# Seven products instead of eight for the other half of the second FFN product as well, with weight sums made in place

## The reference

```python
u = jnp.einsum('bsd,df->bsf', x, w_in)            # 2048 -> 2 * 5632
c = conv_b + up[:, 0:S] * conv_w[0] ...           # causal, width 3
g, val = jnp.split(c, 2, axis=-1)
return jnp.einsum('bsf,fd->bsd', jax.nn.gelu(g) * val, w_out)   # 5632 -> 2048
h = layer_norm(DEEPNORM_ALPHA * h + f, ...)
```

## Time and profile before

| what | value |
|---|---|
| median of three runs | 2568.05 us |
| the profiled execution's own time | 2568.06 us |
| its span | 2566.3 us |
| TensorE busy (matmul) | 2552.7 us, 99% of the span |
| VectorE busy | 1697.4 us, 66% |
| ScalarE busy | 1235.3 us, 48% |
| DMA | 496.05 MB, mean 193 GB/s |

### The profile page before, as it was taken

The page is one execution under the profiler, slowest core; times in us unless marked ns, Lnnn a source line. Parts: engine busy times, 40 slices in busy tenths (PEclk is TensorE's granted clock), DMA queues, the critical chain, the costliest instruction groups (busy, mean ns, idle before and its releaser), DMA issues.

```text
span 2566.3 us, 40343 instructions
## 1 busy us (share of the span) xinstructions
PE 2552.7 (99%) x14286; PEld 2227.7 (87%) x14286; DVE 1697.4 (66%) x1922; ACT 1235.3 (48%) x1383; POOL 15.9 (1%) x39
## 2 busy tenths in 40 slices
PE   9999999999999999999999999999999999999998
PEld 9999888888888888888888888888888888888887
DVE  6666667767666796565555555554766767678955
ACT  4444445555555554434444344433455555555532
POOL 0000000000000000000000000000000000000000
PEclk9999999999999999999999999999999999999999
DMA  7554574555555656655555555566555555556464
GB/s 280 178 172 164 181 251 145 196 192 196 196 192 192 207 219 210 217 177 182 180 180 178 185 180 179 185 212 199 171 193 187 197 193 196 196 193 224 175 230 153
DMA packets 142032, 496.05 MB, mean 193 GB/s; under 512 B 15616, under 2 KB 17920, under 8 KB 141952
## 3 DMA queue, kind: packets, MB, share of 16 engines
q1 hardware_dynamic: 133344, 481.22, 56.0%
q10 hardware_dynamic: 8608, 13.73, 1.6%
HBM read 492.80 MB, written 2.10 MB: 193 GB/s over the span
## 4 chain that ended last, share of the span: by engine, by line
PE 99%; DVE 0%; DMA 0%; SPq 0%; POOL 0%; issue 0%; ACT 0%; DVEq 0%; POOLq 0%; ACTq 0%
PE acc_cm L522 12%; PE acc_ab L522 11%; PE acc_ab L421 11%; PE acc_ab L420 11%; PE acc_ab L418 11%; PE acc_cm L525 6%; PE acc_ab L525 6%; PE acc_ab L435 4%; PE acc_ab L432 4%; PE acc_ab L434 4%; PE acc_cm L418 3%; PE acc_cm L421 3%; PE acc_cm L420 3%; PE acc_cm L688 1%; PE acc_cm L689 1%; PE acc_cm L687 1%
## 5 line engine op out<-in xcount | busy, mean ns | idle before, releaser
L1121 DVE TENSOR_TENSOR w_lo<-raw,w_hi 128x1024 fp32r<-128x1024 f32 x862 | 1045.4, 1223 | 678.3 <-ACT w_hi L797 673.0
L797 ACT ACTIVATE w_hi<-raw 128x1024 fp32r<-128x1024 f32 (+1 forms) x866 | 901.9, 1054 | 753.7 <-PE acc_ab L421 344.3
L522 PE MATMUL acc_cm<-x_parts,w_hi 128*128 128x512 f32 x1408 | 480.1, 389 | 0.0
L522 PE MATMUL acc_ab<-x_parts,w_hi 128*128 128x512 f32 x1280 | 436.2, 389 | 0.0
L525 PE MATMUL acc_cm<-x_parts,w_lo 128*128 128x256 f32 x1408 | 388.6, 276 | 0.0
L525 PE MATMUL acc_ab<-x_parts,w_lo 128*128 128x256 f32 x1280 | 353.3, 276 | 0.0
L522 PEld LDWEIGHTS acc_cm<-x_parts,w_hi 128*128 128x128 f32 x1408 | 264.3, 188 | 54.9
L432 PE MATMUL acc_ab<-x_parts,w_hi 128*128 128x256 f32 x1020 | 284.7, 279 | 1.3 <-DVE x_parts L1150 0.9
L522 PEld LDWEIGHTS acc_ab<-x_parts,w_hi 128*128 128x128 f32 x1280 | 240.2, 188 | 50.0
L435 PE MATMUL acc_ab<-x_parts,w_lo 128*128 128x256 f32 x1020 | 282.0, 276 | 0.0
L434 PE MATMUL acc_ab<-x_parts,w_hi 128*128 128x256 f32 x1020 | 282.0, 276 | 0.0
(11 more groups left out here) (199 smaller groups left out, 3251.1 us busy)
## 6 DMA issues: line engine op xcount, KB each, us to landing
raw<-in_weights_dram SPq DMA_DIRECT2D x878, 512.0 KB, 4.1
pair_raw<-in_weights_dram SPq DMA_DIRECT2D x32, 512.0 KB, 5.4
ln_gain<-in_ln_g_dram ACTq DMA_DIRECT2D x16, 256.0 KB, 5.0
ln_bias<-in_ln_b_dram ACTq DMA_DIRECT2D x16, 256.0 KB, 6.4
h<-in_x_dram ACTq DMA_DIRECT2D x4, 512.0 KB, 7.1
x_t<-in_x_by_feature_dram SPq DMA_DIRECT2D x7, 256.0 KB, 8.0
raw<-in_weights_dram SPq DMA_DIRECT2D x4, 256.0 KB, 4.9
decay_sb<-in_decay_tab_dram ACTq DMA_DIRECT2D x1, 1024.0 KB, 7.2
```

The lines of the kernel that those rows point to most:

```text
L522: pe.matmul(acc[:, f], wh[:, k, c], x_parts[:, CK * s + k].rearrange("p a n -> p (a n)"), start=s == 0 and k == 0, stop=False, skip_group_ ...
L797: return act.activation(o, i, ACT.Copy)
L1121: dve.tensor_tensor(wl, raw[:, at % RING], wh.bitcast(F32), ALU.subtract).then_inc(lo_ready, 1)
```

## The change

Blocks 2 and 3 now form a pair of their own, with the same 56 places. Its units stand at 4, 15, 26, 37 (`LEAD` is now a list for each of the four pairs of the kernel).

The four weight sums of a unit are made in place. T1 overwrites B11, T3 overwrites B12, T2 overwrites B22 and T4 overwrites B21. So the order of VectorE's work changes. T1 follows the split of item 1, T3 precedes that of item 2, T2 precedes that of item 3, and T4 follows that of item 3. The memory of `pair_t` becomes a second group buffer (`unit_raw[1]`). A unit's blocks are loaded once the items of the unit before the last are split.

The early chunks leave the ring. Each is loaded by ScalarE's queue into `next_raw` after a unit of the second pair (`load_next`). ScalarE and VectorE split it (`round_next`, `low_next`) behind place `at + 10` of the unit that starts at `at`. TensorE waits for all four (`next_ready`) in `early_product` of stage 2 and at the head of `last_product`. `product` at the head of `last_product` is gone: the second pair's first 48 places stand for it.

The layer norm's parameters are loaded at places 33, 35, 37 and 39 of the second pair. The residual sum of block 3 is already scaled when `last_residual` comes, so that it is a plain sum there.

The diff, cut to its core:

```diff
+LEAD = [[12, 16, 20, 24], [4, 8, 12, 16], [12, 16, 20, 24], [4, 8, 12, 16]]
+UNIT_AT = [[at + ITEMS * u for u, at in enumerate(lead)] for lead in LEAD]
...
-        pair_raw, = views(side_at, ("pair_raw", [P, 4, CK, COLS], F32))
-        pair_t = nc.alloc_sbuf_tensor_at("pair_t", [P, 4, CK, COLS], F32, offset=sums_at)
+        unit_raw = [nc.alloc_sbuf_tensor_at(f"unit_raw{i}", [P, 4, CK, COLS], F32, offset=at)
+                    for i, at in enumerate((side_at, sums_at))]
+        next_raw = nc.alloc_sbuf_tensor_at("next_raw", [P, RING, CK, COLS], F32, offset=arena_at + word * FT * SEQ)
...
+                    if i + 1 in unit_at:                                   # SyncE, load_pairs
+                        u = unit_at.index(i + 1)
+                        if u == 0:
+                            sp.wait_ge(hid_ready, FSTEPS * (layer + 1))
+                        elif u == 1:
+                            sp.wait_ge(sum_ready, UNITS * (layer + 1))
+                        else:
+                            sp.wait_ge(lo_ready, base + unit_at[u - 2] + ITEMS)
+                        if u == UNITS + 1:
+                            sp.wait_ge(pair_sum, TAPS * (2 * layer + 1))
+                        load_unit(base, u, i + 1)
...
-                product(turn, split, acc_b, b_free, used, hid_hi, hid_lo, False, at=HCH, early_at=EARLY_FROM[4][1])
-                pe.wait_ge(lo_ready, early_position(4, RING - 1) + 1)
+                pe.wait_ge(next_ready, 2 * RING)                           # TensorE, last_product
                 for s in range(2 * RING):
                     done = held_chunk(s, acc_b, 0)
...
-                product(q_out + OQ0, HCH, acc_a, a_free, n_out + 1, hid_hi, hid_lo, False)
                 if not last:
-                    product(q_out + OQ0, HCH, acc_b, b_free, nb_out + 1, hid_hi, hid_lo, False, at=HCH,
-                            early_at=EARLY_FROM[2][1], held=held_units(2))
+                    pair_product(1, q_out + PQ, n_out + 1, nb_out + 1, nc_in + FSTEPS, PAIR - RING, held_units(2))
                 else:
-                    last_product(q_out + OQ0, nb_out + 1)
+                    pair_product(3, q_out + PQ, n_out + 1, nb_out + 1, nc_in + FSTEPS, PAIR - 2 * RING)
+                    last_product(q_out + PQ)
...
+                pair_stream(second, q_out + PQ, LAST_CHUNK[stage] - RING,  # ScalarE
+                            merged({UNIT_AFTER[second]: [copy_p1]}, ln_slots(stage, UNIT_AT[second][2] + ITEMS),
+                                   {at + ITEMS - 1: [lambda s=s: load_next(s)] for s, at in enumerate(UNIT_AT[second])}),
+                            {at + ITEMS + RING - 1: [lambda s=s: round_next(s)] for s, at in enumerate(UNIT_AT[second])})
...
+                def split_item(pair, turn, u, m):                          # VectorE
+                    i = UNIT_AT[pair][u] + m
+                    for t in {2: [T3], 3: [T2]}.get(m, ()):
+                        weight_sum(pair, turn, u, t)
                     wh, wl = parts(i % RING, TOKENS)
-                    dve.wait_ge(hi_ready, RING * q_out + i + 1)
-                    dve.tensor_tensor(wl, whole, wh.bitcast(F32), ALU.subtract).then_inc(lo_ready, 1)
+                    dve.wait_ge(hi_ready, RING * turn + i + 1)
+                    dve.tensor_tensor(wl, unit_raw[u % 2][:, (B11, B21, B22, B11, B12, B22, B21)[m]], wh.bitcast(F32),
+                                      ALU.subtract).then_inc(lo_ready, 1)
+                    for t in {1: [T1], 3: [T4]}.get(m, ()):
+                        weight_sum(pair, turn, u, t)
...
+                def low_next(s):
+                    dve.wait_ge(next_hi_done, RING * layer + s + 1)
+                    eh, el = early[stage]
+                    dve.tensor_tensor(el[:, s], next_raw[:, s], eh[:, s].bitcast(F32),
+                                      ALU.subtract).then_inc(next_ready, 1)
...
+                pair_stream(second, q_out + PQ, LAST_CHUNK[stage] - RING, assembled(second),
+                            {at + ITEMS + RING - 1: [lambda s=s: low_next(s)] for s, at in enumerate(UNIT_AT[second])})
```

More of the change, by code:

```diff
@@ L103, in item_of, with plain_of, stage_item, skipped @@
     return None
[L106 to L116, removed]
+def plain_of(pair, i):
+    n, p = divmod(i - ITEMS * sum(at + ITEMS <= i for at in UNIT_AT[pair]), PLAIN_BLOCK)
+    return n, 2 * UNITS + p
+def stage_item(layer, i):
+    for pair in (2 * layer, 2 * layer + 1):
+        at = i - PAIR * (pair % 2)
+        if 0 <= at and item_of(pair, at) is not None:
+            return item_of(pair, at)
+    return None
+def skipped(layer, i):
+    return sum(stage_item(layer, j) is not None for j in range(i % RING, i, RING))
+def loaded_before(layer, i):
     j = i - RING
-    while j >= 0 and item_of(j) is not None:
+    while j >= 0 and stage_item(layer, j) is not None:
         j -= RING
@@ L705, in pair_product @@
                         pe.wait_ge(hid_ready, FSTEPS * layer + chunk // 2 + 1)
-                    pe.wait_ge(lo_ready, RING * q_out + i + 1)
+                    pe.wait_ge(lo_ready, count(i))
                     for t in range(TT):
-                        last = multiply_tile((acc_a, acc_b)[n], t, parts(i % RING, TOKENS), hid_hi, hid_lo, CK * chunk,
-                                             p == 0 and (n, t) != (1, 0))
+                        last = plain_tile(i, t)
                     last.then_inc(products, 1)
+                if held is not None:
+                    for i in range(chunks, PAIR):
+                        pe.wait_ge(lo_ready, count(i))
+                        done = plain_tile(i, 0)
+                    done.then_inc(first_tile, 1)
+                    for i in range(chunks, PAIR):
+                        plain_tile(i, 1).then_inc(products, 1)
+                        for step in held.get(PAIR - i, ()):
+                            step()
@@ new lines, in round_item, with pair_stream @@
+                        copy(wh, unit_raw[u % 2][:, b]).then_inc(hi_ready, 1)
+                    else:
+                        act.wait_ge(t_ready, 4 * (UNITS * pair + u) + m - 2)
+                        b = (B11, B12, B22, B21)[m - 3]
+                        copy(wh, unit_raw[u % 2][:, b]).then_inc(hi_ready, 1)
+                def pair_stream(pair, turn, chunks, slots, behind):
+                    for s in range(chunks):
+                        act.wait_ge(products, RING * turn + s + 1)
@@ L1560, in pair_stream, with assembled @@
+                def assembled(pair):
+                    after = UNIT_AFTER[pair]
+                    return {after: [lambda: add_first_block(pair)], after + 1: [lambda: add_p5_p6_p1(pair)],
+                            after + 2: [lambda: add_p7(pair)], after + 3: [lambda: first_stats(pair)]}
+                def pair_stream(pair, turn, chunks, slots, behind):
+                    for s in range(chunks):
+                        dve.wait_ge(products, RING * turn + s + 1)
                         for step in slots.get(s, ()):
@@ L1725, in weight_stream @@
     parts += with_early(rwo, 3, w_in[1][0]) + up(1)
-    split = HCH - 2 * RING
-    last = w_out[1][NBLK - 1]
-    parts += with_early(pair(w_out[1])[:-1] + [last[:split], last[split + RING:]], 4, last[split:split + RING])
+    held = PAIR - 2 * RING
+    ahead = w_out[1][NBLK - 1][HCH - 2 * RING:HCH - RING]
+    first, second = paired(w_out[1], 1, ahead)
+    parts += [first, second[:held], second[held + RING:]]
     return np.ascontiguousarray(np.concatenate(parts, axis=0))
```

347 lines of the change are left out of this document (177 added, 170 removed).

## The result

The changed kernel takes 2573.93 us (median of 12 runs, 2573.14 to 2575.22), the kernel before 2568.22 (12 runs, 2567.48 to 2568.85). The ratio is 1.0023, 95% interval 1.0014 to 1.0032: 5.7 us slower, inside the range given and 4.4 us above the time given. The profiled execution took 2574.53 us with a span of 2572.7.

A forecast was written before the change was run, and what follows sets the result against it. TensorE, busy 99% of the span, was taken as the bound, others mattering only where it waits. -10.88 + 0.5 + 7.2 + 4.6 = +1.4 us on 2568.06 gave 2569.5 us; own range 2567 to 2572, 8-in-10 range 2562 to 2575.

The forecast's parts named there:

- Rival 2: VectorE's chain to item 4 lacks slack: all 16 units lose 0.3 to 0.4 us more, +5.6, 2575.1 us; chance 0.10.
- rival 3: TensorE's clock falls in the 4.6 us gap; half speed behind it loses up to 3.6 us, 2573.1 us; chance 0.10.
- no change: Whole kernel: 0.2%, 5.1 us, is about what a measurement can tell from no change; chance of same 0.71.
- The matmuls removed: TensorE, blocks 2 and 3: 24 fewer matmuls in each of two layers, 48 x 0.2267 = 10.88 us saved.
- Ten bare units: Item 4 of units without an early-chunk split ahead: 0 to 0.2 us lost each, 0.05 taken, 0.5 us in all.
- self-waits: VectorE sums T3 and T2 each wait for their direct predecessor, taken to start 0.04 us after its end.
- Six units with `low_next`: Units 1 to 3 of second pairs: an early-chunk split delays item 4 by 1.2 us each, 7.2 us (6.3 to 7.6).
- bare chain: VectorE's splits 1 to 4 and four sums, eight instructions ahead of item 4, with 0.09 us of slack.
- The gap at the end: Head of layer 1's last eight chunks: TensorE waits for the late fourth early chunk, 4.6 us (3.9 to 5.1).
- The clock: TensorE behind the gap in layer 1: half speed after idling, up to 3.6 us, held outside the sum as rival 3.
- Costed at nothing: Early chunks' splits and copies, 16 sums and second assembly per layer, moved parameter loads and weight loads: 0 us of their own.

The follow-up runs named there:

- all-three kernel: Changed kernel with ring chunks first in the last eight, three early chunks split five places later, and weight sums one step earlier: 2558.21 us, ratio 0.9962.
- kernel with one instruction more: Changed kernel plus an unused VectorE reduction of 1.21 us behind T4 in the eight units of the first pairs: 2583.01 us, ratio 1.0058.
- sums' experiment: Changed kernel with each weight sum one step earlier, behind the split of the item before: 2569.36 us, ratio 1.0005.
- last experiment: The all-three kernel with the four parameter loads at places 40, 42, 44 and 46 instead of 33 to 39: 2559.40 us, ratio 0.9966.

## Why the prediction was right or wrong

The time lies in the range, but only because the range was drawn around rivals 2 and 3: it is above the forecast's own range (2567 to 2572), and at 5.7 us it lies beyond the 5.1 that I had called no change. So the range was hit with a sum that lacked one term.

- **The matmuls removed, -10.88.** Right: 48 fewer. In the all-three kernel, where the waits are almost gone, 9.9 us of it arrive, and the account leaves 1.1 us of waits.
- **Ten bare units, +0.5; measured 1.9** (0.19 each, at the top of my 0 to 0.2, which was put together from other parts: I had 0.14 for the handoff and 0.07 behind it, and measured are 0.02 of lateness, 0.05 and 0.11; that these come to much the same is luck). The chain was taken 0.1 us too short: an instruction that waits for the one before it started 0.09 us after its end (923.14 to 923.23), and I had 0.04 from the earlier trace rows. The size is not what makes the difference: with the sums earlier, instructions of the full size too start 0.03 to 0.04 us after the one they wait for, also where that one was queued. What does make it isn't shown. With two of these the slack is -0.02 instead of 0.09 us. From there on every unit pays the restart. I chose 0.05 because the sum ended ahead of the need; a sum with 0.09 us to spare and two unmeasured handoffs should have been taken in the middle. Moving the sums took the ten waits out, which shows the chain to be their cause: VectorE then stands idle between the splits of a bare unit. It doesn't tell the self-waits from the count of instructions ahead of split 4; that two self-waits cost 0.17 us each in the changed kernel is read from its rows alone.
- **Six units with `low_next`, +7.2; measured 8.0.** Right in place, in the number of units and in the mechanism; in size above the 6.3 to 7.6 that I had given, because the restart costs 0.11 instead of 0.07 and the bare chain already had no slack. 1.33 each, of which 1.14 is the instruction (gone when it is moved, and the same when another is put in) and 0.19 the bare chain.
- **The gap at the end, +4.6; measured 4.4.** Right, and so are its steps: from the first assembly step to the split behind the stats VectorE took 10.47 us (2524.16 to 2534.63) where I had 10.46. VectorE is never idle in the gap, and the last `early_lo` releases TensorE.
- **The clock.** I left it out of the sum and put it down as rival 3 with a chance of 0.10 and a price of up to 3.6. It came, at 2.8 us. The same rival gave 2573.1 as the time, and the median is 2573.93; it is that near because its 3.6 us was 0.8 too high and the 1.4 and 0.8 us above were not in it. This is the step that failed: an omitted term, next in size to the gap itself. The trace of before has no such gap, and I let a mechanism without a row stay out of the sum, although its price could be bounded and its condition, the gap, was in my own forecast. The Trainium skill ("TensorE: Matmul & The Clock Gate", section "HAM oscillation — how this bites in real kernels") says that a long idle gap between matmuls sends the clock back down and that the engine then restarts cold. Here the traces agree: the clock fell in idle times of 4.4 and 5.6 us, and held where the gap was filled. In the kernel with one instruction more it fell just after the matmuls had started again.
- **Rival 2, that all sixteen units lose 0.3 to 0.4 us.** Of its 5.6 us came 1.4 + 0.8 = 2.2, those above: its self-waits did cost 0.05 us more each, the sums in place cost nothing more.
- **Costed at nothing.** The weights' loads were: they land after a median of 8.4 us instead of 5.4, and no wait of ScalarE, VectorE or TensorE names one. The parameter loads are covered only while VectorE is late; the sums' experiment uncovered them at unit 3.

By terms: -10.9 + 1.9 + 8.0 + 4.4 + 2.8 = +6.2 where I had +1.4. Of the 4.8 between them 2.8 are the clock, 1.4 the bare units, 0.8 the long ones, less 0.2 at the gap.

## What to carry to other kernels

A count of instructions saved on the bounding engine doesn't give the time until the in-order queue that feeds it has been added up at its tightest point, an instruction at a time; with no slack, every instruction more cost its full queued time there, and moving three things by a few places took this kernel from 2573.9 to 2558.2 us. Read the bounding engine by start-to-start distances, because the waits of 0.07 us and the slow matmuls of this case stood in no list of waits. When a gap of some microseconds opens on TensorE, price the slow matmuls behind it too, and ask first whether work that is ready can stand ahead of the wait. And when loads are moved, look for what else is loaded in the new place: in the last experiment a chunk's weights landed 4 us later than before.

## What the runs showed of the hardware

- After TensorE had stood idle for 4.4 us (5.6 in another kernel) its granted clock was 0.50 and equal matmuls lay 0.43 us apart instead of 0.227, the first pair 0.59, for 5.7 us (4.4). In the kernel with one instruction more, after 4.4 us too, the clock fell 0.4 us behind the restart and the slow stretch was 3.4 us. So its length did not follow the gap's. Behind idle times of 0.43 and 1.05 us the clock stayed at 1.00.
- On VectorE, two 128x1024 instructions queued without a wait start 1.14 us apart at a duration of 1.22. One that waits for its predecessor starts 0.09 us after its end in the changed kernel, 1.31 us apart, so such a wait costs 0.17 us; with the sums one step earlier it starts 0.03 to 0.04 us after it, at a cost of 0.12 us. The Trainium skill ("VectorE: DVE Perf Modes", section "The DRAIN you can't avoid") reports of eight copies that a semaphore after each cost nothing extra over one after the last. Here the rows have a cost of 0.12 to 0.17 us, and for these instructions they decide.
- TensorE starts 0.05 us after the end of the split that releases it (927.87 to 927.92), and the second matmul behind such a release is 0.11 us late (0.34 us start to start at full clock), so here a split that ended 0.02 us too late cost 0.19 us.
